# A hybrid decoder layer on eight cores: the pooling branch's map and scale folded into the output weight

## The reference

```python
def _pool_mixer(p, w_pool, pool_scale):
    ...
    for gi, w in enumerate(POOL_WINDOWS):
        ...
        outs.append((cs[:, :, sl] - lower) / count - pf[:, :, sl])
    pooled = jnp.stack(outs, axis=2)                             # (B, T, G, Dg)
    mixed = jnp.einsum('btgc,gcd->btgd', pooled, w_pool.astype(jnp.float32))
    return mixed.reshape(B, T, D_POOL) * pool_scale.astype(jnp.float32)
...
        mix = jnp.concatenate([o_rec, o_pool], axis=-1) @ w_out[l].astype(f32)
        h = h + gt_a * mix
```

## Time and profile before

| | us |
|---|---|
| median of three runs | 2979.76 |
| the three runs | 2970.16, 2979.76, 3490.82 |
| the profiled execution | 2967.67 |
| its span, slowest core | 2966.1 |
| the spans of its eight cores | 2953.0 to 2966.1 |

### The profile page before, as it was taken

The page is one execution under the profiler, slowest core; times in us unless marked ns, Lnnn a source line. Parts: engine busy times, 40 slices in busy tenths (PEclk is TensorE's granted clock), DMA queues, the critical chain, the costliest instruction groups (busy, mean ns, idle before and its releaser), DMA issues.

```text
span 2966.1 us, 47124 instructions; the slowest of 8 cores (2953.0 to 2966.1 us)
## 1 busy us (share of the span) xinstructions
PE 2748.4 (93%) x16352; PEld 1374.5 (46%) x16352; DVE 1750.3 (59%) x3398; ACT 1374.7 (46%) x2327; POOL 154.4 (5%) x258
## 2 busy tenths in 40 slices
PE   3156987999999999999999999999999999999997
PEld 1033533545454544545454554545454454545443
DVE  2135653757566665757666575757666575757642
ACT  3023533536365554626455553627455553627330
POOL 2000110000000000000000000000000000000000
PEclk9566999999999999999999999999999999999999
DMA  9984999669675857767585857768584857767453
GB/s 197 166 153 76 209 203 217 218 175 227 181 237 153 242 153 204 215 178 234 173 233 160 232 176 194 221 176 236 169 240 154 229 188 188 224 174 210 128 180 126
DMA packets 344921, 567.06 MB, mean 191 GB/s; under 512 B 176224, under 2 KB 225632, under 8 KB 344688
## 3 DMA queue, kind: packets, MB, share of 16 engines
q1 hardware_dynamic: 267680, 430.11, 50.6%
q0 software_dynamic: 77008, 133.94, 20.6%
HBM read 504.39 MB, written 57.70 MB: 190 GB/s over the span
## 4 chain that ended last, share of the span: by engine, by line
PE 87%; DMA 7%; DVE 2%; another core or an unknown queue 2%; issue 1%; ACT 1%; POOL 0%; SPq 0%; DVEq 0%; POOLq 0%; ACTq 0%
PE pb L480 86%; DMA wsl<-w_in 3%; DMA wsl<-wup_s 1%; DMA wsl<-w_down 1%; DVE S L497 1%; DMA ucT<-xn 1%; DMA koutk<-koutT 1%; DMA wsl<-w_up 0%; DMA wsl<-win_s 0%; DMA wup_s<-wsl 0%; ACT rsb L486 0%; DVE xh L494 0%; DVE pb L494 0%; POOL hidT L503 0%
## 5 line engine op out<-in xcount | busy, mean ns | idle before, releaser
L480 PE MATMUL pb<-u2T,wsl 128*128 128x512 bf16 x4096 | 940.7, 381 | 7.8 <-DMA wsl<-wup_s 2.9
L480 PE MATMUL pb<-wsl,hidT 128*128 128x512 bf16 x4096 | 903.8, 380 | 15.7 <-DMA wsl<-w_down 13.6
L480 PEld LDWEIGHTS pb<-wsl,hidT 128*128 128x128 bf16 x4096 | 397.9, 98 | 500.5 <-issue 30.6
L480 PEld LDWEIGHTS pb<-u2T,wsl 128*128 128x128 bf16 x4096 | 390.7, 98 | 454.9 <-issue 27.7
L490 DVE TENSOR_SCALAR pb<-pb 128x512 f32<-128x512 f32 x512 | 357.2, 698 | 257.3 <-PE pb L480 254.7
L480 PE MATMUL pb<-wsl,ucT 128*128 128x256 bf16 (+1 forms) x3072 | 482.1, 313 | 14.0 <-DVE S L497 6.3
L486 ACT ACTIVATE hidT<-pb 128x512 bf16<-128x512 f32 x512 | 306.1, 598 | 386.5 <-DVE pb L490 345.6
L480 PEld LDWEIGHTS pb<-wsl,ucT 128*128 128x128 bf16 x3072 | 299.8, 99 | 178.5 <-issue 36.8
L480 PE MATMUL pb<-ucT,wsl 128*128 128x512 bf16 x1536 | 348.7, 386 | 7.8 <-DVE ucT L491 4.3
L494 DVE TENSOR_TENSOR pb<-pb,gbc 128x512 f32<-128x512 f32 x256 | 173.9, 696 | 280.9 <-PE pb L480 280.3
L497 DVE SCALAR_TENSOR_TENSOR S<-S,decs,pb 128x128 f32<-128x128 f32 x1024 | 286.4, 343 | 16.6 <-DVE S L497 7.2
(11 more groups left out here) (94 smaller groups left out, 1817.6 us busy)
## 6 DMA issues: line engine op xcount, KB each, us to landing
wsl<-wup_s SPq DMA_DIRECT2D x240, 512.0 KB, 3.8
wsl<-wdn_s SPq DMA_DIRECT2D x240, 512.0 KB, 3.8
wsl<-win_s SPq DMA_DIRECT2D x150, 512.0 KB, 5.8
xh<-x POOLq DMA_DIRECT2D x64, 512.0 KB, 8.3
out<-xh POOLq DMA_DIRECT2D x64, 512.0 KB, 7.0
wsl<-wout_s SPq DMA_DIRECT2D x60, 512.0 KB, 6.6
fg<-x POOLq DMA_DIRECT2D x28, 512.0 KB, 8.7
qs<-x POOLq DMA_DIRECT2D x28, 512.0 KB, 9.8
```

The lines of the kernel that those rows point to most:

```text
L480: return lambda e: e.matmul(out, lhsT=lhsT, rhs=rhs, start=start, stop=stop, **k)
```

## The change

The map and the scale are multiplied into the weight instead of into the activations. At the start `wpool`, now laid out transposed, is loaded as fp32 into `rsb` on SP's queue, and four DVE products scale it into the tile `wpool`. In the first round of `ring_mix`, `fold_pool` replaces the 512 pooling rows of `w_out` (pieces 1 and 3, four groups each) by map times rows, through four PSUM banks and an ACT or DVE copy back into the slot, before the piece is stored to scratch. Later tiles load the folded pieces. `pool_j`'s DVE copy now writes the means straight into `ucT`, rows 4 to 7, as four runs of 128 columns, and `pool_g` is gone from every tile. Also gone is `plv`, the view of `Et`.

```diff
@@ -572,7 +571,10 @@
-        cload("pool", "wpool", wpool, wpool_d, 262144)
+        P.dma("sp", dm(rsb[:], wpool_d.ap()), writes=[B_rsb], key="c_wpool", nbytes=262144)
+        for g in range(4):
+            P.dve(ts(V(wpool, g * 128, [[1, 128]]), V(rsb, g * 128, [[1, 128]]), V(psc, g, [[1, 1]]), None, ALU.mult),
+                  reads=[B_rsb] + C("psc"), writes=C("wpool"), dur=0.2)
@@ -595,6 +597,16 @@
+        def fold_pool(i):
+            for g in range(4):
+                bk = mix_bank()
+                P.pe([mm(pb[bk][:], V(wpool, g * 128, [[1, 128]]), W4(i, g), True, True)], reads=[B_w[i]] + C("wpool"),
+                     writes=[B_pb[bk]], dur=MM)
+                if g % 2 == 0:
+                    P.act(actf(W4(i, g), pb[bk][:], AF.Copy), reads=[B_pb[bk]], writes=[B_w[i]], dur=0.6)
+                else:
+                    P.dve(cp(W4(i, g), pb[bk][:]), reads=[B_pb[bk]], writes=[B_w[i]], dur=0.69)
@@ -609,6 +621,8 @@
                     P.dma("pool", dm(V(wsl[i], 0, dims), src), writes=[B_w[i]], key="cw%d" % i, nbytes=1048576, dur=0.9)
+                    if kind == "wout" and pc % 2 == 1:
+                        fold_pool(i)
                     P.dma("sp", dm(scr[kind].ap()[pc], wsl[i][:]), reads=[B_w[i]], writes=[B_scr[kind][pc]],
@@ -801,14 +815,8 @@
-                P.dve(cp(plv(j * 512, [[1, 512]]), pb[bp][:]), reads=[B_pb[bp]], writes=[B_E[j // 2]], dur=0.69)
-
-            def pool_g(g):
-                bx = 6 + g % 2
-                P.pe([mm(V(pb[bx], 0, [[128, 4], [1, 128]]), V(wpool, g * 128, [[1, 128]]), plv(g * 128, [[512, 4], [1, 128]]),
-                         True, True)], reads=B_E + C("wpool"), writes=[B_pb[bx]], dur=MM)
-                P.act(actf(V(ucT, (4 + g) * TT, [[1, TT]]), pb[bx][:], AF.Copy, scale=V(psc, g, [[1, 1]])),
-                      reads=[B_pb[bx]] + C("psc"), writes=B_uc[4 + g], dur=0.69)
+                P.dve(cp(V(ucT, 4 * TT + j * 128, [[TT, 4], [1, 128]]), V(pb[bp], 0, [[128, 4], [1, 128]])), reads=[B_pb[bp]],
+                      writes=[B_uc[4 + g][j] for g in range(4)], dur=0.69)
@@ -858,8 +866,6 @@
-            for g in range(4):
-                pool_g(g)
```

More of the change, by code:

```diff
@@ L348, in build_nc @@
     gnw_d = din("gnw", [128, 1])
-    wpool_d = din("wpool", [128, 4, 128])
+    wpool_d = din("wpool", [128, 512])
     psc_d = din("psc", [128, 4])
@@ L423, in build_nc @@
         ddv = lambda i, off, dims: cast(xn, F32, (2 + i) * TT + off, dims)
-        plv = lambda off, dims: cast(Et, BF16, off, dims)
         pbb = lambda i, off, dims: cast(pb[i], BF16, off, dims)
@@ L989, in make_in_maps @@
         "gnw": f(np.asarray(inputs["g_norm_w"], np.float32)[0].reshape(128, 1)),
-        "wpool": f(np.asarray(inputs["w_pool"], np.float32)[0].transpose(1, 0, 2)),
+        "wpool": f(np.asarray(inputs["w_pool"], np.float32)[0].transpose(2, 0, 1).reshape(128, 512)),
         "psc": f(np.asarray(inputs["pool_scale"], np.float32)[0].reshape(4, 128).T),
```

## The result

The kernel after takes 3009.61 us (median of four runs, 3001.14 to 3355.11), the kernel before 3143.73 on the same chip (median of four, 2970.16 to 3490.82); both lists hold some disturbed runs, which the ratio leaves out: **1.0112, 95% interval 1.0067 to 1.0158**. The change makes the kernel some 1.1% slower. The prediction was 2964 with a range of 2945 to 2984, a gain of 0.3%.

What follows compares the result with a forecast made beforehand. PE was taken as the bound, 97% of a tile's period being matmul columns. Tile 0 +7.0, tile 1 -3.0, steady tiles -12.1 gave -8.1 us on 2967.67: 2959.6, or about 2964 as a median; range 2945 to 2984.

Steps and rivals of the forecast that it cites:

- the part on steady tiles: Tiles 2 to 15: four matmuls fewer per tile, moved copies add no wait; 12.1 us gained, bounds 0 to 17.8.
- Tile 1: In the DMA stretch: chain 5.3 us shorter without the map; 3.0 us gained, bounds 0 to 5.3.
- PE's gap is refilled: Rival, steady tiles: weight stream or a wait takes over, gain there lost; 2971.7 us (2976.5 as a median), chance 0.07.
- The last rival: DMA stretch: the planner's new order adds one 10.59 us wait for a late load; 2970.2 us (2975), chance 0.07.
- The columns: Tiles 2 to 15: four 512-column matmuls fewer per tile at 0.2158 us each; 12.1 us gained.
- Tile 0: State products start earlier, gaining 3.67 us; the fold delays stage C; 7.0 us lost net of that gain.
- The lower bound, 5.6: Tile 0: least net loss from the fold, in us, with no stage C matmul at half clock.
- the four-step form: Tile 0's fold: four serial steps per weight piece, 6.3 us, piece 3 beside piece 1 one step behind.
- the half-clock rival: Tile 0's stage C stays at 1.2 GHz, 8.4 us more; 2970.1 us (2975 as a median), chance 0.07.
- the eight-step rival: Tile 0's fold runs all eight steps one after another, 13.3 us lost; 2966 us (2971), chance 0.12.
- The small parts: Kernel start: later `wpool` queueing, DVE products, staging and stores cost nothing; bound 0.5 us for `wpool`.
- The list of what would show it: Signs in the profile after, among them 56 fewer matmuls, tile period near 168.0, UP at about 278 us.

Runs made afterwards that it cites:

- e10: Kernel after with 6 us more planned for koutk landings, the fold in banks 2 and 3, and 16 extra 512-column matmuls a tile; ratio to before 1.0162.
- e12: Kernel before with koutT transposed by PE and copied by ACT in every tile instead of by DMA; ratio to before 1.0037.
- e13: Kernel after with koutT transposed by PE in every tile and the fold in banks 2 and 3; ratio to before 0.9954.
- e3: Kernel after without the fold, so the pooling map and scale are left out of the computation; ratio to before 1.0069.
- e1: Kernel after with a planner that takes the koutk transposes as landing 6 us later; ratio to before 1.0003.

## Why the prediction was wrong

**The failed step** stands at the end of the part on steady tiles: "The copies no longer wait for `Et` ... no wait is added." It looked for the inputs of what was moved, the copies. The state products are what moved most: they came 5.3 us closer to the last transpose, and their other operand `koutk` was never listed. The data was there: the DMA issues of before give 8.4 us as the median landing of all these transposes, SP's queue gives the issue of head 3's (1043.88), PE's timeline the use (1056.60). 12.7 less 5.3 is 7.4 us, under that median and further under head 3's own of 9.4. With head 3's landings one by one, as the trace of before has them, and the 0.25 us from landing to product that the rows of after show, products that come 5.3 us earlier wait in 12 or 13 tiles of 15, for an estimated 29.9 to 37.1 us on each of the eight cores; after has 12 or 13 waits of 25.9 to 36.6 us. Tile 1's working left out the same operand: on six of the eight cores its state products wait for it too, from 0.5 to 4.9 us.

**The rival that came true** was "PE's gap is refilled: ... a wait takes over in the steady tiles", with a chance of 0.07. Its price was the real error: it was put at the lost gain (2971.7), as if a wait could at most fill the gap that the map left. A wait has the size of what is late, 2.55 us here and up to 4.6 on this core, and nothing ties it to the 0.86 us removed; and the lower clock adds to it. The steady tiles came out at +34 us instead of -12.1. The last rival, "The planner's new order puts a product behind a late load", had the mechanism too, but counted one wait in the DMA stretch and not one in nearly every tile; an order that stalls in every tile was named only with the 0.02 for a loss of over 2%.

**The columns** (-12.1) were right as a price: e10 measured 0.205 each, with a wide interval, e12 and e13 0.98 us a tile for four, which also holds whatever else the change does there. "97% of the period is columns, so a column removed is time removed" holds where nothing else is uncovered by the removal.

**Tile 0.** The gain came: the state products start 0.14 us after the last cast's end (198.94 + 1.29 to 200.37). The fold was priced at 7.0 net of 3.67, so 10.7 from state products to UP; measured 9.9 (after against e3) and 8.7 (after against before). UP came 7.5 us later on average over the cores, against the 7.0. (The lower bound, 5.6, comes to 5.8 by its own terms, which changes nothing.) Its start was predicted at 242.2 with stage C at 248.5, and they came at 242.28 and 248.18. It was the four-step form, with the second piece one step behind; the clock rose within stage C (60 matmuls in 14.61 us), so the half-clock rival and the eight-step rival fall.

**Tile 1** (-3.0). The runs don't give it alone: e12 and e13 differ by 7.3 us from tile 0's state products to tile 2's, which holds it, the hidden fold and the earlier state products. There is a gain in these tiles, but the share of tile 1 in it is not separated.

**The small parts** were right. `wpool` landed 10.8 us after its issue, the four DVE products took 16.39 to 19.04, and `modT` came at 43.95 still behind 22.26 us of waiting for PE: nothing was late for it. The DVE cast in four runs takes 0.68 us, as taken.

**The list of what would show it** named the sign itself: "Wrong if the tile period stays 168.9". It was predicted near 168.0, was 167.95 in before already on average (the 168.89 of the earlier trace rows was one tile, with a wait of 1.24 us in it), and became 170.35. So a period of 168.0 would not have told the forecast from no change at all.

## What to carry to other kernels

Cheap instructions between a transfer's issue and its use are cover for the landing, however little of the engine they take. Before removing some, list for the next instruction on that engine every operand with issue, landing time and the new time of use; take the landings of that very transfer, not those of its whole kind, and where they don't fit, count a wait for each one that misses, with everything queued behind it, and not just the gain that is lost. An order written by a planner inherits its landing estimate: a removal that shortens the path turns an estimate that was harmless into stalls.

## What the runs showed of the hardware

A wait in a dense stretch of matmuls can cost more than itself: behind waits of 2.55 and 4.59 us the granted clock over the next 8 us was 0.80 and 0.73, and 32 matmuls took 8.38 us instead of 7.07; behind one of 1.00 us it stayed at 1.00, and on another core also behind one of 3.50 us. A DMA transpose of a 128x512 bf16 tile, issued in the same place of every tile (head 3's), landed after 3.8 to 13.1 us in before, median 9.4. Sixteen PE transposes a tile with four ACT copies cost the steady tile about 1 us (tiles without waits: 167.3 in before, 168.4 in e12; 166.5 in e1, 167.3 in e13), less than the 2 us a tile that PE waited for DMA transposes in after (29.7 us in 15 tiles). Four DVE products of 128x128 with one scalar a partition took 2.65 us at the start of the kernel, 0.58 each on average, where 0.2 were taken in the plan.
